# Waits of the expert passes moved to the product they guard, a scatter cut in two, wider gaps between tiles

## What is computed

```
mix_l = y @ w_o                                   # 1024 x 1024: the unit "wo2"
x_lat = x_lat + g1 * mix_l
t = modulate(rmsnorm(x_lat, norm2_g), sh2, sc2)   # h2
lg, le = t @ w_rg + b_rg, t @ w_re + b_re         # router: 4 groups, 16 experts
gates = ...                                       # best group, best two of its four experts
for e in experts:
    y = (silu(t @ w1[e]) * (t @ w3[e])) @ w2[e]
    acc = acc + gates[e] * y
out = rmsnorm(x_lat + g2 * acc, final_g)
```

## Time and profile before

| what | us |
|---|---|
| median of 3 runs (lowest, highest) | 1209.31 (1208.77, 1213.37) |
| the profiled execution | 1205.35 |
| its span | 1203.2 |
| TensorE busy | 1153.4 (96%) |
| VectorE, ScalarE busy | 663.2 (55%), 499.2 (41%) |
| granted TensorE clock, mean of the span | 0.988 |

### The profile page before, as it was taken

The page is one execution under the profiler, slowest core; times in us unless marked ns, Lnnn a source line. Parts: engine busy times, 40 slices in busy tenths (PEclk is TensorE's granted clock), DMA queues, the critical chain, the costliest instruction groups (busy, mean ns, idle before and its releaser), DMA issues.

```text
span 1203.2 us, 21401 instructions
## 1 busy us (share of the span) xinstructions
PE 1153.4 (96%) x8936; PEld 996.9 (83%) x8936; DVE 663.2 (55%) x1143; ACT 499.2 (41%) x797; POOL 87.0 (7%) x92
## 2 busy tenths in 40 slices
PE   7999899999999989999999999999999899999996
PEld 6998789998979969999979889767899766665764
DVE  5777875588866476665555342775557531221223
ACT  5766523644374555544445222667344311111112
POOL 2451320000000100000100000000002000000000
PEclk9999999999999999999999999999999899999998
DMA  9544240443514746555564321302857899999980
GB/s 368 206 143 175 71 176 1 141 154 131 189 54 152 270 176 245 189 196 184 202 245 175 116 94 71 141 2 114 340 181 299 335 422 421 420 420 420 422 366 36
DMA packets 36204, 254.59 MB, mean 212 GB/s; under 512 B 4048, under 2 KB 4192, under 8 KB 5904
## 3 DMA queue, kind: packets, MB, share of 16 engines
q1 hardware_dynamic: 33552, 237.84, 51.4%
q0 software_dynamic: 2560, 15.42, 3.3%
HBM read 252.19 MB, written 1.05 MB: 210 GB/s over the span
## 4 chain that ended last, share of the span: by engine, by line
PE 85%; DVE 9%; ACT 3%; issue 2%; DMA 0%; DVEq 0%; ACTq 0%
PE bank L1374 13%; PE bank L712 12%; PE bank L706 12%; PE bank L707 12%; PE bank L668 5%; PE bank L1096 5%; PE bank L1182 4%; PE bank L1103 3%; PE bank L1386 2%; PE bank L759 2%; PE bank L1406 2%; PE bank L728 1%; PE bank L883 1%; DVE ring_low L2101 1%; PE bank L1284 1%
## 5 line engine op out<-in xcount | busy, mean ns | idle before, releaser
L2101 DVE TENSOR_TENSOR ring_low<-ring,w_high 128x2048 fp32r<-128x2048 f32 x104 | 238.0, 2290 | 160.8 <-ACT w_high L1629 160.7
L1629 ACT ACTIVATE w_high<-ring 128x2048 fp32r<-128x2048 f32 x104 | 199.1, 1915 | 281.5 <-PE bank L712 192.9
L706 PE MATMUL bank<-nT_high,w_high 128*128 128x256 f32 (+1 forms) x448 | 114.6, 295 | 0.0
L706 PEld LDWEIGHTS bank<-nT_high,w_high 128*128 128x128 f32 x448 | 84.2, 188 | 2.6 <-issue 2.4
L1374 PE MATMUL bank<-more,xs 128*64 128x256 f32 x768 | 84.6, 379 | 0.0
L1374 PEld LDWEIGHTS bank<-more,xs 128*64 128x64 f32 x768 | 58.7, 137 | 25.7 <-issue 2.2
L706 PE MATMUL bank<-hcl,w_high 128*128 128x256 f32 (+1 forms) x272 | 73.1, 306 | 0.0
L707 PE MATMUL bank<-hcl,w_high 128*128 128x256 f32 (+1 forms) x272 | 71.2, 299 | 0.0
L707 PE MATMUL bank<-nT_low,w_high 128*128 128x256 f32 (+1 forms) x272 | 64.7, 280 | 0.0
L706 PE MATMUL bank<-nMs,w_high 128*128 128x256 f32 x256 | 60.3, 280 | 1.4 <-DVE nMs L2493 1.4
L1096 PE MATMUL bank<-up,w_high 128*128 128x256 f32 x512 | 60.7, 276 | 0.0
(11 more groups left out here) (565 smaller groups left out, 2479.5 us busy)
## 6 DMA issues: line engine op xcount, KB each, us to landing
ring<-stream SPq DMA_DIRECT2D x163, 1024.0 KB, 4.9
more<-stream SPq DMA_DIRECT2D x60, 1024.0 KB, 18.7
more<-stream POOLq DMA_DIRECT2D x10, 1024.0 KB, 15.0
c<-constants_one SPq DMA_DIRECT2D x1, 1657.0 KB, 16.2
qc<-h_in SPq DMA_DIRECT2D x4, 272.0 KB, 3.8
c<-constants_two POOLq DMA_DIRECT2D x1, 1056.0 KB, 9.0
beside<-stream POOLq DMA_DIRECT2D x1, 1024.0 KB, 13.0
hT<-h_in POOLq DMA_DIRECT2D x1, 1024.0 KB, 6.0
```

What stands on the lines that cost most here:

```text
L706: nc.tensor.matmul(into[j], w, high_x(k), start=first, stop=False, skip_group_check=True)
L1629: A(w_high[:, d % 2, :], ring[:, s, :], ACT.Copy).then_inc(high_ready, 1)
L2101: TT(ring_low[:, s, :], ring[:, s, :], w_high[:, d % 2, :], sub).then_inc(low_ready, 1)
```

## The change

Six things change.

1. `STAGGER` goes from 16 to 48 words, and a third filler stands before `y_dsa`. The tiles behind the first filler move by 128 bytes, those behind the second (`hcl`) by 256, those behind the new one (`y_dsa` and what follows it) by 320; `w_high`, `ring` and `ring_low` stay. The distance from the moving tile to the weights, in bytes modulo 256, as the built programs place them:

| moved tile | to `w_high`, before | now | to `ring_low`, before | now |
|---|---|---|---|---|
| `nMs`, `up`, `heads`, `merged2`, `four` (high and low) | 192 | 64 | 96 | 224 |
| `y_gdn` high / low | 192 / 192 | 64 / 64 | 96 | 224 |
| `merged` high / low | 192 / 64 | 64 / 192 | 96 | 224 |
| `y_dsa` high / low | 128 / 0 | 64 / 192 | 32 | 224 |
| `hcl` | 64 | 64 | 224 | 224 |
| `hcl` as weights, `w_high` moved (line 1182) | 192 | 192 | 32 | 32 |
| `nT` (272 wide) | every multiple of 64 in turn | the same, two blocks further on | in turn | in turn |

2. The router's blocks 0 to 5 move from the middle of the last `wo2` unit into its first part, ahead of the row blocks k = 0, 1, 2, 3, 5 and 7; only the square of block 5 stays in the middle.
3. In each pass the down products wait for `hid_ready` alone; `gate_slot_ready` is awaited ahead of q = 1.
4. In the first pass the choices are turned ahead of the hidden rows.
5. The trip's head no longer waits for `gates_loaded`; that wait stands at the gate products.
6. `scatter` waits for each half of `yb` at the first product that reads it. In the trip, blocks 0 to 3 are scattered ahead of the up products and blocks 4 to 7 behind them; the last scatter behind the loop also waits half by half.

```diff
-STAGGER = 16
+STAGGER = 48
...
+                _stagger_dsa = sb(m, "stagger_dsa", 128, STAGGER)
                 with ExitStack() as same:
                     y_dsa_low = sbr(same, "y_dsa_low", 128, H, SEQ)
...
                 for k in range(KT):
                     k_ready(k)
+                    among(k)
...
                 elif u == 3:
-                    router_blocks(range(6))
+                    router_squares([5])
+
+            def among_wo2(u, k):
+
+                blocks = {0: [0], 1: [1], 2: [2], 3: [3], 5: [4], 7: [5]}.get(k)
+                if u == 3 and blocks:
+                    router_blocks(blocks)
...
-            def scatter(count, signal=False, first=False):
-
-                pe.wait_ge(ys_ready, count * 2 + 2)
-                pe.wait_ge(spread_ready, count + 1)
-                for ft in range(KT):
+            def scatter(count, signal=False, first=False, fts=range(KT)):
+
+                if fts[0] == 0:
+                    pe.wait_ge(spread_ready, count + 1)
+                for ft in fts:
+                    if ft % 4 == 0:
+                        pe.wait_ge(ys_ready, count * 2 + 1 + ft // 4)
...
                     gather_blocks(range(KT), 2 * CAP)
-                    scatter(count - 1)
+                    scatter(count - 1, fts=range(4))
...
+                if first:
+                    turn_choices()
+                    turn_hidden()
+                else:
+                    scatter(count - 1, first=(n == 1), fts=range(KT) if n < PAIRS else range(4, KT))
+                    turn_hidden()
+                    turn_choices()
...
                 pe.wait_ge(hid_ready, count + 1)
-                pe.wait_ge(gate_slot_ready, count * 2 + 2)
                 for q in range(2):
+                    if q == 1:
+                        pe.wait_ge(gate_slot_ready, count * 2 + 2)
...
             with pe.Fori(0, extra) as x:
-                pe.wait_ge(gates_loaded, 2 * x + 2)
                 expert_pass(PAIRS, x, x + PAIRS, lambda qt: gate_of[:, qt, :])
```

More of the change, by code:

```diff
@@ L694, in low_parts, with split_tiles @@
                 pe.wait_ge(low_ready, d + 1)
-            def split_tiles(kind, u, high_x, low_x, n, names, k_ready=lambda k: None, halfway=lambda: None, drains=1):
+            def split_tiles(kind, u, high_x, low_x, n, names, k_ready=lambda k: None, halfway=lambda: None, drains=1, among=lambda k: None):
                 s, cnt, d, (high_w, low_w) = split_unit(kind, u)
@@ L1317, in router_blocks, with router_squares @@
                                          start=(k == 0 and qt == 0), stop=False, skip_group_check=True)
-                if blocks[0] == 0:
-                    pe.wait_ge(partial_ready, 3)
-                for k in blocks[-1:] if blocks[0] == 0 else blocks:
+            def router_squares(blocks):
+                dst = psum[banks.at["router"]]
+                pe.wait_ge(partial_ready, 3)
+                for k in blocks:
                     if k >= 6:
@@ L1346, in _ @@
                 split_tiles("wo2", u, lambda k: merged2_high[:, k, :], lambda k: merged2_low[:, k, :], SEQ, [("wo2", u)],
-                            lambda k: pe.wait_ge(merged2_ready, k // 2 + 1) if u == 0 else None, lambda: between_wo2(u), drains=0)
+                            lambda k: pe.wait_ge(merged2_ready, k // 2 + 1) if u == 0 else None, lambda: between_wo2(u), drains=0,
+                            among=lambda k: among_wo2(u, k))
             router_blocks(range(6, KT))
+            router_squares(range(6, KT))
             pe.wait_ge(h_ready, 3 * KT)
@@ L1435, in expert_pass, with turn_hidden, turn_choices @@
                     gather_blocks(range(KT), 2 * CAP)
-                    scatter(count - 1)
+                    scatter(count - 1, fts=range(4))
                     for q in range(2):
                         half_rows(n, again, 2 * q, psum[q][:, 0:256], xs[:, :, 0:2 * CAP], KT, UNIT_COLS, rows_ready if q == 0 else lambda k: None)
[L1439 to L1446, removed]
-                    nc.tensor.transpose(psum[3][:, qt * 128:(qt + 1) * 128], pick_again[:, qt, :], ident)
-                group(psum[3][:, SEQ:SEQ + 2], [(pick_again[:, qt, :], gates(qt)) for qt in range(2)]).then_inc(spread_full, 1)
+                def turn_hidden():
+                    pe.wait_ge(hid_rows_ready, count + 1)
+                    for k in range(4 if n < PAIRS else 2):
+                        last = nc.tensor.transpose(psum[2][:, k * 128:(k + 1) * 128], hid_rows[:, k * 128:(k + 1) * 128], ident)
+                    last.then_inc(hid_full, 1)
+                def turn_choices():
+                    pe.wait_ge(again_ready, count * 4 + 4)
+                    for qt in range(2):
+                        nc.tensor.transpose(psum[3][:, qt * 128:(qt + 1) * 128], pick_again[:, qt, :], ident)
+                    if n == PAIRS:
+                        pe.wait_ge(gates_loaded, 2 * again + 2)
+                    group(psum[3][:, SEQ:SEQ + 2], [(pick_again[:, qt, :], gates(qt)) for qt in range(2)]).then_inc(spread_full, 1)
+                if first:
[5 more added lines that the diff above has]
+                    turn_choices()
                 if n == 0:
```

2 lines of the change are left out of this document (1 added, 1 removed).

## The result

| | kernel before | changed kernel |
|---|---|---|
| median of the timed runs, us | 1210.34 (1208.77 to 1213.37, 4 runs) | 1192.61 (1191.56 to 1194.20, 4 runs) |
| ratio, 95% interval | | 0.9852 [0.9828, 0.9875] |
| the profiled execution, us (span, mean granted clock) | 1205.35 (1203.2, 0.988) | 1194.20 (1192.0, 0.989) |

The two profiled executions differ by 11.2 us only.

What follows compares the result with a forecast made beforehand. TensorE, 96% busy, was taken to bound the kernel, so shortening its products or pauses pays. The terms summed to 10.55, say 10.6 us, off the median 1209.3: 1198.7 us, 8 in 10 for 1193.5 to 1203.5.

Steps and rivals of the forecast that it cites:

- trip's head and clock: Extra trip's start: gather no longer waits for gate_of, 1.5 us gained; without that pause no half-speed clock, 3.1 us.
- scatter, trip and tail: Half the scatter moves behind the trip's up products, 0.55 us; half the last scatter fills its wait for yb_low, 1.05.
- gate slot, pairs and trip: Down products start without waiting for gate_slot: 0.58 us in each of four odd pairs, 2.3 us; 0.7 in the trip.
- first pass: Turning the choices fills TensorE's wait for the hidden rows in the first pass: 0.55 us gained.
- router: Its 24 small rows cost 2.75 us among wide products as in a row; 0.1 us lost.
- gaps, against an execution with the quick MLP: Moved tiles' new distances: 0.6 us from ring_low groups, 0.3 from heads; 0.9 gained, bounds 2.1 gained to 4.6 lost.
- signs that the prediction named against itself: A load wait at pair 7's down products, an xs wait at the trip's up products, or a longer dense part to 934 us.
- The step that failed: Setting the 10.6 us sum against the runs' median, 1209.3 us, rather than the profiled 1205.35: 1198.7 instead of 1194.8.
- 1024 x 4.5 ns = 4.6 us: Bound of the gaps: loss if the products of nMs and up take the slow spacing at their new distances.
- No worse by its median: Gaps: most tiles move to distance 64, where hcl had a median of 276 ns, from one with both prices.

Runs made afterwards that it cites:

- experiment 4: Kernel before, only the extra trip's wait for its gate values moved to the product that reads them; median 1200.81 us, ratio 0.9929.
- experiment 5: Changed kernel, the extra trip's wait for its gate values put back at the loop's head; median 1198.99 us.
- experiment 6: Changed kernel, scatter whole again, behind a wait for both halves of its rows and ahead of the trip's up products; median 1193.62 us.
- experiment 7: Changed kernel, gate slot awaited ahead of all down products and first pass turning hidden rows ahead of choices again; median 1196.28 us.
- experiment 8: Changed kernel, the router's six blocks together in the middle of the last unit again; median 1193.37 us.
- experiment 1: Kernel before, run again with no edit; median 1207.71 us over 12 executions, ratio 1.0007.
- experiment 2: Kernel before with the wider gaps alone (STAGGER 48 and the filler before y_dsa); median 1203.67 us, ratio 0.9959.
- experiment 9: Kernel before, each gap 256 bytes wider, so distances modulo 256 stay as they were; median 1209.99 us.
- experiment 10: Kernel before with 32 words ahead of w_high (MLP: 192 to w_high, 224 to ring_low); median 1210.50 us.
- experiment 11: Changed kernel with 32 words ahead of w_high (MLP: 64 to w_high, 96 to ring_low); median 1196.49 us.
- experiment 12: Changed kernel, gaps wider by another 256 bytes (the one ahead of y_dsa stays), same distances modulo 256; median 1191.58 us.
- experiment 13: Changed kernel with 8 words ahead of w_high (64 to w_high, 192 to ring_low); median 1191.24 us, ratio to before 0.9848.
- experiment 14: Changed kernel with 24 words ahead of w_high (64 to w_high, 128 to ring_low); median 1195.11 us.

## Why the prediction was right and wrong

| term | forecast, us | measured, us | read from |
|---|---|---|---|
| trip's head and clock | 1.5 + 3.1 | 5.06 and 5.09 | experiments 4, 5 |
| scatter, trip and tail | 0.55 + 1.05 | 0.57 + 0.79 | experiment 6 |
| gate slot, pairs and trip | 2.3 + 0.7 | 2.48 + 0.79 | experiment 7 |
| first pass | 0.55 | 0.67 | experiment 7 |
| router | -0.1 | -0.14 | experiment 8 |
| gaps, against an execution with the quick MLP | 0.9 | 1.0 | profiles of experiments 1, 2, 20 to 926 us: 0.4 lost to 288 us, 1.4 gained behind it |
| sum | 10.6 | 11.2 | |
| gaps, against an execution with the slow MLP | not in the sum | 4.8 more | experiment 4 |

**The mechanisms held.** The pause at the head was 1.8 us and went in full: the loop's entry is hidden behind the products issued ahead. The clock did fall because of the pause. VectorE's `xs` came in time, so nothing waits for it. None of the signs that the prediction named against itself came in the profile after. The sum of the parts, 11.2 us, agrees with the 11.2 between the two profiles; of these 10.4 are the passes and the end, while the last 0.7 hold falls of the clock at other places too, so that there the agreement may be chance.

**The step that failed** is the last one: "The median of the runs shown is 4.0 us above that execution, with the same work; I set the sum against the median". It is the same work, but not at the same rate. The profile came from the group of executions whose MLP runs at 113.4 ns, while two of the three runs shown, 1209.31 and 1213.37 us, lie in the other group, and the third at its edge. The gaps remove that group: of 43 executions of kernels with the changed kernel's distances in the MLP none shows it, eight by their profiles (113.3 ns), the rest by span times clock. So the change takes 4.8 us from every execution that has it, and the term of the gaps should have been 0.9 us and 4.6 times a chance. I had both prices, "1024 x 4.5 ns = 4.6 us", but put it down as a loss that the new distances might bring, and left out that the old ones might bring it in executions that I hadn't seen. The rows hinted at it: `nMs` at 276 and `heads` at 279 with the same distance, which I read as a matter of how a unit began and then didn't ask whether the MLP always begins alike.

Account: from 1209.3 or 1210.3 us, 11.2 for the sum and, as the medians of before lie in the upper group, 4.8 for the MLP make 16.0 of 16.7 or 17.7 measured. What is left, up to 1.7 us, is within what the clock's other falls vary by: in the 17 profiles they stand at different places (at 13 and 440 us in most, at 142 and 166 in others, in and behind the router 6.8 to 13.7 us in all). What brings those about stays open; the move of the router's blocks may have a part (experiment 8). The prediction overlooked them: it calls the trip the only place where TensorE stands idle and then runs slowly, but its own profile shows 0.50 twice between 942 and 953 us too, behind the router.

**The distances.** "No worse by its median" was right, and for the tiles that ran at both prices the forecast held: the median of `heads_high` is 276, that of `y_dsa_high` hardly moved. The rows by tile of line 708 after, beside the earlier trace rows:

```profile
L708 PE MATMUL bank<-nMs,w_high x256: 276/276/436, 438.4 to 528.2; 128*128 128x256 f32 x128
...
L708 PE MATMUL bank<-y_dsa_high,w_high x64: 280/281/367, 360.3 to 397.7; 128*128 128x256 f32 x64
...
L708 PE MATMUL bank<-heads_high,w_high x64: 276/276/384, 841.5 to 891.7; 128*128 128x256 f32 x64
```

So the pair isn't the whole rule either: `y_dsa_high` now has the MLP's 64 and 224 and stays at 281. Its low tile, moved in turn with it, stands at 192 by the table; whether that is why, no run tells.

The Trainium skill, "TensorE: Matmul & The Clock Gate", "Part 2: What happens when you issue a matmul", says that loading the next weights takes no read bandwidth of SBUF from the running product. By it alone experiments 2, 9 to 11 and 12 to 14, which move tiles and nothing else, should all give the time of their base. They give medians from 1203.7 to 1210.5 us on the kernel before, and 113.4 or 117.8 ns for one product. Here the measurement decides: place matters. Why it does, no run shows.

## What to carry to other kernels

A profile is one execution. Before a sum is set against a median, compare the profiled time with the runs: where it lies outside them, or at their end, ask which part of the program can run at two rates, and give that a chance of its own; span times mean granted clock tells quickly whether the clock explains the distance. Put a wait at the product that reads the guarded value: besides the wait itself, a pause of 1.8 us of TensorE cost 3.3 us more in the clock behind it. Where hundreds of equal products follow one another, compare their mean spacing between tiles and executions; a filler of a few words between tiles can be worth as much as a wait (4.8 us here in the executions that it changes, 5.1 for the trip's wait).

## What the runs showed of the hardware

- Products of one shape (128x128 loaded, 256 columns moved, 4 bytes) run at 113.4 or 117.8 ns for a whole stretch of 32 units, and which of the two can differ between executions of one program (two groups, 4.8 us apart), at a granted clock of 1.00. By the MLP's pair of distances (to `w_high`, to `ring_low`, modulo 256): 192 and 96, by their times the longer in 41 of 76 executions; 192 and 224, none of 12 under 1208.9 us; 64 and 96, the longer in 2 of 6; 64 and 224, in none of 43; 64 and 192, in none of 5, with the groups of `ring_low` at 113.1 instead of 116 ns.
- Small products take a wide product's place: four rows of 20 columns between wide ones cost 0.46 us, 0.115 each, as in a row.
- A pause of 1.8 us of TensorE ahead of the trip was followed by 6.83 us at 0.50 in six of six profiles; without the pause the clock stayed at 1.00 there in eleven of eleven.
- One execution to the next, the same program's clock falls at other places: mean 0.983 to 0.990 in 76 executions of the kernel before.
